# Head norms of a recurrent layer: sums kept in 18 rows, factors spread by a store and repeated-row loads in place of matrix products

## The reference, cut to what matters

```python
kk = (k * k_k).reshape(B, T, H, E)
kk = kk / jnp.maximum(jnp.sqrt(jnp.sum(kk * kk, axis=-1, keepdims=True)), 1e-12)
...
mean = jnp.mean(y, axis=-1, keepdims=True)
var = jnp.mean(jnp.square(y - mean), axis=-1, keepdims=True)
yn = (y - mean) * lax.rsqrt(var + LNX_EPS) * lnx_w.reshape(H, E) + lnx_b.reshape(H, E)
```

## Time and profile before

| | |
|---|---|
| runs | 1655.82, 1649.14, 1655.05 us, median 1655.05 |
| profiled execution | 1649.22 us, its span 1647.4 us |
| TensorE busy | 1530.8 us, 93% of the span |
| VectorE / ScalarE / GpSimd busy | 678.1 / 425.5 / 54.8 us |
| mean granted TensorE clock | 0.979 of full |
| recurrent part | from about 63 to 620 us |

### The profile page before, as it was taken

How to read it: one execution, slowest core, us unless ns; L and a number is a source line. 1 busy time by engine, 2 the same in 40 slices (tenths; PEclk the granted TensorE clock), 3 DMA queues, 4 the chain that set the end, 5 groups by cost and what they waited for, 6 DMA issues and landing times. The chain is left out here.

```text
span 1647.4 us, 32642 instructions
## 1 busy us (share of the span) xinstructions
PE 1530.8 (93%) x13954; PEld 1038.5 (63%) x13954; DVE 678.1 (41%) x1669; ACT 425.5 (26%) x876; POOL 54.8 (3%) x57
## 2 busy tenths in 40 slices
PE   7898999999999998998989989999999999995997
PEld 4565676676776656675766664555786777772442
DVE  5456375466455225325152452324552111113554
ACT  4411414313422212314132240113111111111444
POOL 0000000000000000000000000000110011002110
PEclk9999999999999999999999999999999999997998
DMA  5100000100010107405243284004699999995321
GB/s 197 29 27 2 26 17 16 41 15 16 16 42 10 42 10 304 193 16 208 100 194 128 92 346 167 39 26 179 245 359 351 383 375 372 382 397 189 102 90 45
DMA packets 55606, 238.39 MB, mean 145 GB/s; under 512 B 7584, under 2 KB 18080, under 8 KB 45728
## 3 DMA queue, kind: packets, MB, share of 16 engines
q1 hardware_dynamic: 45776, 201.63, 32.1%
q0 software_dynamic: 6176, 22.02, 4.3%
q10 hardware_dynamic: 3504, 12.58, 1.9%
HBM read 206.53 MB, written 29.69 MB: 143 GB/s over the span
## 5 line engine op out<-in xcount | busy, mean ns | idle before, releaser
L466 PE MATMUL bank<-h,w 128*128 128x352 f32 (+1 forms) x528 | 183.8, 496 | 0.0
L466 PEld LDWEIGHTS bank<-h,w 128*128 128x128 f32 x528 | 100.2, 199 | 55.5 <-issue 7.4
L1942 PEld LDWEIGHTS bank<-cache,we 128*128 128x128 f32 x1088 | 125.0, 194 | 11.8 <-issue 7.2
L1942 PE MATMUL bank<-cache,we 128*128 128x96 f32 (+1 forms) x1088 | 126.3, 277 | 3.4 <-DVE cache L2273 3.4
L2273 DVE COPY cache<-bank 128x512 f32<-128x512 f32 (+1 forms) x54 | 31.6, 626 | 217.4 <-PE bank L1921 217.1
L2551 PE MATMUL bank<-we,unT 128*128 128x512 f32 x256 | 112.9, 599 | 1.4 <-DVE unT L2502 1.4
L1864 PE MATMUL bank<-cache,mixed 128*128 128x512 f32 x256 | 112.7, 599 | 0.0
L1354 PE MATMUL bank<-h,w 128*128 128x352 f32 (+1 forms) x288 | 88.4, 469 | 0.0
L2551 PEld LDWEIGHTS bank<-we,unT 128*128 128x128 f32 x256 | 48.6, 193 | 59.5 <-issue 57.8
L1864 PEld LDWEIGHTS bank<-cache,mixed 128*128 128x128 f32 x256 | 48.7, 193 | 58.7 <-issue 58.7
L1964 PE MATMUL bank<-we,gated 128*96 128x512 f32 (+2 forms) x192 | 79.5, 595 | 0.0
(11 more groups left out here) (427 smaller groups left out, 2561.1 us busy)
## 6 DMA issues: line engine op xcount, KB each, us to landing
we<-in_weg SPq DMA_DIRECT2D x24, 1024.0 KB, 14.8
we<-in_weu SPq DMA_DIRECT2D x24, 1024.0 KB, 17.8
we<-in_wed SPq DMA_DIRECT2D x24, 1024.0 KB, 20.3
cache<-in_kcj SPq DMA_DIRECT2D x4, 5120.0 KB, 16.1
cache<-in_vcj SPq DMA_DIRECT2D x4, 5120.0 KB, 15.7
cache<-in_weg SPq DMA_DIRECT2D x8, 1024.0 KB, 15.6
cache<-in_weu SPq DMA_DIRECT2D x8, 1024.0 KB, 18.9
cache<-in_wed SPq DMA_DIRECT2D x8, 1024.0 KB, 19.9
```

The costliest lines, as they stand in the source:

```text
L466: mm = pe.matmul(out[:, 0:w], w3[:, KIND[q], kd, :], g.uT[:, kd, a:a + w], start=(kd == 0), stop=(kd == KD - 1))
L1942: mm = pe.matmul(bank[6 + u % 2][:, 128 * (2 * a + f):128 * (2 * a + f) + CAPS[e]], weights[load_of[e] % NW][a][:, k, 128 * f:128 * f + 12 ...
```

## The change

In the stages that have an own pair (j = 0 to 3) both norms are made in another form; the first and the last stage keep the old one.

- `sums_in_rows`: the squares stream (128 columns a block) over a strip of zeros with one column of ones per head, shifted by one column from block to block, so all nine blocks accumulate into one bank: row tt holds head 0's sums of block tt, row 9 + tt head 1's. Scaling, root and reciprocal work on [18, 128].
- `spread_rows` on SP: when the reciprocal is made, two stores put the 2 x 9 rows into DRAM; when these have landed, two loads bring each head's 1088 values to its 64 partitions, the same DRAM row read 64 times.
- Norm rows lie in `tmp`, their spread in `bv`; key rows in `bv`, their spread in `tmp`. DVE multiplies once over 1088 columns from there. The reuse brings waits: ACT waits for the norm stores before it squares the keys into `tmp`, and for the norm multiplication and the key stores before it evicts into `bv`.
- On SP the norm's trip stands behind the load of k weights, the key's behind the store of output rows (and a small load), and ahead of the loads of r and v weights.
- On DVE the key reciprocal moves ahead of the `z16` read and the second r shift ahead of the key multiplication. PE loses its waits for `d_rec`, `a_rec` and `d_bcx` in these stages.

```diff
@@ sync
+                def spread_rows(rows, out, made, n, stored, landed):
+                    sp.wait_ge(s[made], n)
+                    sp.dma_start(g.rows[0, :, :], rows[0:TT, :]).then_inc(s[stored], 16)
+                    sp.dma_start(g.rows[1, :, :], rows[TT:2 * TT, :]).then_inc(s[stored], 16)
+                    uses[stored] += 32
+                    sp.wait_ge(s[stored], uses[stored])
+                    for h in range(2):
+                        row = g.rows[h, :, :].rearrange("a t -> (a t)")[0:T].unsqueeze(0)
+                        sp.dma_start(out[hs(h), :], row.broadcast_to([E, T])).then_inc(s[landed], 16)
...
                     if jn is not None:
                         next_w3("k", jn)
+                    if jp is not None and j < J:
+                        spread_rows(norm_rows, norm_spread, "d_rec", jp + 1, "n_stored", "n_landed")
                     if jp is not None:
                         sp.wait_ge(s["g_ev"], 3 * jp + 3)
                         sp.dma_start(g.rw[128 * jp:128 * jp + 128, :], cen).then_inc(g.rw_out, 16)
...
+                    if jn:
+                        sp.wait_ge(s["n_landed"], 32 * j)
+                        spread_rows(key_rows, key_spread, "a_rec", jn + 1, "k_stored", "k_landed")
@@ tensor
+                def sums_in_rows(of, out):
+                    order = (0, TT - 1) + tuple(range(1, TT - 1))
+                    for tt in order:
+                        n = rows_of(tt)
+                        mm = pe.matmul(out[0:2 * TT, 0:n], strip[:, TT - 1 - tt:3 * TT - 1 - tt], of[:, 128 * tt:128 * tt + n],
+                                       start=(tt == order[0]), stop=(tt == order[-1]))
+                    return mm
...
-                            head_sums(squares, bank[3]).then_inc(s["d_var"], 1)
-                    if behind:
+                            (sums_in_rows if own else head_sums)(squares, bank[3]).then_inc(s["d_var"], 1)
+                    if behind and not own:
                         pe.wait_ge(s["d_rec"], jp + 1)
                         for part in range(3):
                             spread(stat, bank[NORM_SPREAD[part]], part).then_inc(s["d_bc"], 1)
...
-                        if ahead and n == 3:
+                        if ahead and not own and n == 3:
                             pe.wait_ge(s["a_rec"], jn + 1)
...
@@ scalar
+                        if behind:
+                            act.wait_ge(s["n_stored"], 32 * (jp + 1))
                         act.activation(tmp[:, :], kk[:, :], ACT.Square).then_inc(s["a_sq"], 1)
...
                     if own:
+                        if behind:
+                            act.wait_ge(s["d_bcx"], jp + 1)
+                        if ahead:
+                            act.wait_ge(s["k_stored"], 32 * jn)
                         side(("bv", 0))
@@ vector
+                    if behind and own:
+                        dve.wait_ge(s["n_landed"], 32 * (jp + 1))
+                        dve.scalar_tensor_tensor(out=cen[:, :], in0=cen[:, :], scalar=param("lnx_w", jp), in1=norm_spread, op0=ALU.mult,
+                                                 op1=ALU.mult).then_inc(s["d_bcx"], 1)
...
+                        if own:
+                            shift_in(jn, "r", 1)
+                            dve.wait_ge(s["k_landed"], 32 * jn)
+                            dve.tensor_tensor(kk[:, :], kk[:, :], key_spread, ALU.mult)
```

More of the change, by code:

```diff
@@ L283, in rwkv @@
         w0s = sb("w0s", [128, 2, NB, NT])
-        stat, kstat = (g.mixed[:, spare + a:spare + a + 2 * TT] for a in (0, 2 * TT))
+        stat = kstat = g.mixed[:, spare:spare + 2 * TT]
+        strip = g.mixed[:, spare + 2 * TT:spare + 2 * TT + 3 * TT - 1]
         rest = sb("rest", [128, 3 * J])
@@ L608, in between @@
                     jn, jp = after(j), before(j)
-                    ahead, behind = jn is not None, jp is not None
+                    ahead, behind, own = jn is not None, jp is not None, 0 <= j < J
                     def group(n):
@@ L655, in between @@
                             pe.wait_ge(s["a_sq"], jn + 1)
-                            if behind:
-                                pe.wait_ge(s["d_bcx"], 3 * jp + 1)
-                            head_sums(tmp, bank[7]).then_inc(s["a_ss"], 1)
-                        if ahead and n == 3:
+                            (sums_in_rows if own else head_sums)(tmp, bank[7]).then_inc(s["a_ss"], 1)
+                        if ahead and not own and n == 3:
                             pe.wait_ge(s["a_rec"], jn + 1)
-                            if behind:
-                                pe.wait_ge(s["d_bcx"], 3 * jp + 3)
                             for part in range(3):
@@ L920, in between @@
                         act.wait_ge(s["d_eps"], jp + 1)
-                        act.activation(stat[:, :], stat[:, :], ACT.Sqrt).then_inc(s["d_root"], 1)
+                        rows = norm_rows if own else stat[:, :]
+                        act.activation(rows, rows, ACT.Sqrt).then_inc(s["d_root"], 1)
                     if own:
@@ L940, in between @@
                         act.wait_ge(s["a_max"], jn + 1)
-                        act.activation(kstat[:, :], kstat[:, :], ACT.Sqrt).then_inc(s["a_root"], 1)
+                        rows = key_rows if own else kstat[:, :]
+                        act.activation(rows, rows, ACT.Sqrt).then_inc(s["a_root"], 1)
                     if own:
@@ L1093, in between @@
                         dve.wait_ge(s["d_root"], jp + 1)
-                        dve.reciprocal(stat[:, :], stat[:, :]).then_inc(s["d_rec"], 1)
+                        rows = norm_rows if own else stat[:, :]
+                        dve.reciprocal(rows, rows).then_inc(s["d_rec"], 1)
                     if own:
@@ L1099, in between @@
                         keys(jn, 2)
+                    if behind and own:
+                        dve.wait_ge(s["n_landed"], 32 * (jp + 1))
+                        dve.scalar_tensor_tensor(out=cen[:, :], in0=cen[:, :], scalar=param("lnx_w", jp), in1=norm_spread, op0=ALU.mult,
+                                                 op1=ALU.mult).then_inc(s["d_bcx"], 1)
+                    elif behind:
+                        for n, (a, w) in enumerate(SPANS):
+                            dve.wait_ge(s["d_bc"], n + 1)
+                            dve.scalar_tensor_tensor(out=cen[:, a:a + w], in0=cen[:, a:a + w], scalar=param("lnx_w", jp),
+                                                     in1=bank[NORM_SPREAD[n]][:, 0:w], op0=ALU.mult, op1=ALU.mult)
                     if behind:
[L1101 to L1104 removed]
                         dve.drain()
@@ L1115, in between @@
                         dve.wait_ge(s["a_ss"], jn + 1)
-                        dve.tensor_scalar(kstat[:, 0:16], bank[7][:, 0:16], 1e-24, None, ALU.max)
-                        dve.tensor_scalar(kstat[0:64, 16:18], bank[7][0:64, 16:18], 1e-24, None, ALU.max).then_inc(s["a_max"], 1)
+                        if own:
+                            dve.tensor_scalar(key_rows, bank[7][0:2 * TT, 0:128], 1e-24, None, ALU.max).then_inc(s["a_max"], 1)
+                        else:
+                            dve.tensor_scalar(kstat[:, 0:16], bank[7][:, 0:16], 1e-24, None, ALU.max)
+                            dve.tensor_scalar(kstat[0:64, 16:18], bank[7][0:64, 16:18], 1e-24, None, ALU.max).then_inc(s["a_max"], 1)
                         shift_in(jn, "r", 0)
+                    if ahead:
+                        dve.wait_ge(s["a_root"], jn + 1)
+                        rows = key_rows if own else kstat[:, :]
+                        dve.reciprocal(rows, rows).then_inc(s["a_rec"], 1)
                     if own:
                         last_chunk("z16", 1)
-                    if ahead:
-                        dve.wait_ge(s["a_root"], jn + 1)
-                        dve.reciprocal(kstat[:, :], kstat[:, :]).then_inc(s["a_rec"], 1)
                     if own:
@@ L1126, in between @@
                     if ahead:
-                        for n, (a, w) in enumerate(SPANS):
-                            dve.wait_ge(s["a_nb"], 3 * jn + n + 1)
-                            dve.tensor_tensor(kk[:, a:a + w], kk[:, a:a + w], bank[KEY_SPREAD[n]][:, 0:w], ALU.mult).then_inc(s["a_nbx"], 1)
+                        if own:
+                            shift_in(jn, "r", 1)
+                            dve.wait_ge(s["k_landed"], 32 * jn)
+                            dve.tensor_tensor(kk[:, :], kk[:, :], key_spread, ALU.mult)
+                        else:
+                            for n, (a, w) in enumerate(SPANS):
+                                dve.wait_ge(s["a_nb"], n + 1)
+                                dve.tensor_tensor(kk[:, a:a + w], kk[:, a:a + w], bank[KEY_SPREAD[n]][:, 0:w], ALU.mult)
                         dve.drain()
                         dve.tensor_tensor(tmp[:, :], kk[:, :], icl[:, :], ALU.mult)
-                        shift_in(jn, "r", 1)
+                        if not own:
```

(6 more changed lines are left out.)

18 lines of the change are left out of this document (10 added, 8 removed).

## The result

The changed kernel takes 1662.4 us (median of 20 executions, 1652.52 to 1667.36); before, measured as often, takes 1652.7 us (1646.99 to 1658.52). The ratio is 1.0054, 95% interval 1.0039 to 1.007: slower by about 9 us, where 1649.4 us was forecast with a range up to 1659. The profiled execution of the changed kernel took 1658.66 us against 1649.22 us of the profiled one before.

The account below looks back on a forecast made before the run. PE's instruction stream was taken as the bound, 93% busy. Keys -6.5, norms +1.1 - 2.2 + 2.5 and sums -0.6 gave -5.7 us, from the median 1655.05 to 1649.4 us, range 1640 to 1659.

Parts of the forecast that it names:

- The sum: Whole kernel: keys -6.5, norms of j = 1, 2, 3 +1.1, -2.2, +2.5, sums -0.6, together -5.7 us.
- the structure: Norm trips: DVE waits at its 1088-column multiplication and PE behind it in j = 1 and 3, not in j = 2.
- the covered stage: Norm of j = 2: the trip is all hidden with 1.5 us to spare, -2.16 us.
- The key half: Keys in j = 0, 1, 2: trips covered by PE's own work, 3 x -2.16 = -6.5 us.
- stalls cost clock: Rival, chance 0.14: PE's stalls in j = 1 and 3 drop its clock, 1.7 us each, 1652.8 us.
- the trip: SP's stores and repeated-row loads after the reciprocal: 5.9 us, between 5.0 and 12 us.
- the repeated-row loads are slow: Rival, chance 0.13: the trip takes 6 us more, giving +10.4 us, 1665.5 us.
- The estimate of 5.7 us beside the sum: The trip's chain by the Trainium skill's DMA figures with second issues; would make the sum 0.4 us lower.
- removed products: Six spreads dropped from PE, keys j = 0 to 2 and norms j = 1 to 3: 6 x 2.16 = 13.0 us gain.
- products kept PE slow: Rival, chance 0.14: after key sums of j = 1 and 2, 128-column sums could keep the clock, -3.4 us, 1646.0 us.

Follow-up runs that it names:

- bare delays: Four kernels: the kernel before with idle VectorE operations ahead of the third gm pair in stage 1, 3 or both, no trip; +5.9, +7.4, +12.9 and +29.5 us.
- best1: The changed kernel with norms new in stages 1 and 2 only, where SP issues the norm trip ahead of the k weights; 1645.58 us, ratio 0.997.
- nospread: The kernel before with only the key half changed and the norm spread products of stages 1 to 3 left out, no trip replacing them; 1642.06 us, ratio 0.995.
- nowait: The changed kernel with all transfers, but VectorE's norm multiplication in stages 1 to 3 reads an old tile instead of awaiting loaded rows; 1642.77 us, ratio 0.9951.
- n3only: The changed kernel with norm factors by the trip in stage 3 alone, by products in stages 1 and 2; 1652.99 us, ratio 1.0007.
- pair_first: The changed kernel with VectorE's third gm pair ahead of the wait for loaded norm rows in stages 1 to 3; 1655.22 us, ratio 1.0023.
- norm_only: The kernel before with only the output norms of stages 1, 2 and 3 in the new form, keys old; 1660.36 us, ratio 1.007.
- layout: The kernel before with the change's DRAM tensor and four semaphores allocated and never used; 1649.93 us, ratio 0.9999.
- keys_only: The kernel before with only the key norms of stages 0, 1 and 2 in the new form, output norms old; 1645.17 us, ratio 0.997.
- best3: The changed kernel with norm trips ahead of weights in stages 1 and 2, third pair before stage 3's norm wait, first pair before decay's subtraction; 1645.62 us, ratio 0.9958.
- stall_3: The kernel before with five idle VectorE operations ahead of the third gm pair in stage 3 alone; +7.4 +- 2.5 us.
- dvestall: The kernel before with five idle VectorE operations ahead of the third gm pair in stages 1 and 3; +12.9 +- 3.4 us.

## Why the prediction was wrong

The sum said -5.7 us and the measured difference is +9.7. (The three runs shown of before have a median of 1655.05, the longer series 1652.7; this base was 2.4 us high, so the forecast time looks nearer than the sum was.) Three terms failed; by size the third is the largest.

**Right: the structure.** DVE waits at its 1088-column multiplication in j = 1 and 3 and not in j = 2, PE stands at the successor of L572 in the same two, the covered stage is covered. The prediction named the stalls as 3.3 and 4.7 us; they are 4.06 and 6.01. The reciprocal takes 0.93 us (0.95 forecast), the sums hold PE for 1.96 us (285.87 to 287.83; 1.87 to 2.04 forecast). In j = 1 DVE had the rows at 303.04 (302.5 forecast), in part by luck: the loads took 1.3 us more than forecast, but the stores had landed 0.6 us earlier. DVE's wait at the key multiplication is 1.1 us in one stage and PE has none behind it. The key half was to bring 6.5 us and brought 5.3 +- 1.9.

**Wrong, first: the stalls' clock was left out of the sum.** I had the mechanism as a rival (*stalls cost clock*, chance 0.14, 1.7 us for each of two) and took for the forecast that a stall costs its length. The bare delays show length and a quarter: 2.5 us for the 10.07 us of standing here. The evidence was in the earlier trace rows, one window of two after a 2.4 us wait, and stalls of 3 to 5 us are longer than those. That rival belonged in the sum. Alone it would not have saved the forecast: its own figure was 1652.8, still 2.3 us under the base.

**Wrong, second: the trip was sized too short.** The loads were put at 3.8 us from their first issue, from single transfers in the earlier trace rows, and took 5.06 in j = 1 and 5.6 in j = 3; the trip of j = 3 took 7.2 us (537.58 to 544.78) after a start at once. This is 0.8 and 1.3 us more standing, 2.1 together. It is the rival *the repeated-row loads are slow* in its size, not in its cause: 64 different rows took 4.8 and 5.1 us as well. What was left out is that a pair of such loads takes longer than one. The estimate of 5.7 us beside the sum has the same gap; its fit (Trainium skill, "DMA: Bandwidth & Descriptors", "Anatomy of one DMA") is given there for transfers issued by GpSimd, and SP issued these. j = 2 had the spare for it.

**Wrong, third: removed products were credited in full to the span.** Each kernel from which norm spreads went came out above its sum. The sum here is -5.3 for the keys as measured, -2.16 for each norm spread gone, and 1.24 us for each us of standing added in its trace:

| kernel | spreads, standing | by the sum | measured | above |
|---|---|---|---|---|
| best1 | 2, none | -9.6 | -4.7 +- 2.4 | 4.9 |
| nospread | 3, none | -11.8 | -8.3 +- 3.6 | 3.5 |
| nowait | 3, none | -11.8 | -7.6 +- 2.5 | 4.2 |
| n3only | 1, 5.1 | -1.2 | +1.1 +- 2.5 | 2.3 |
| pair_first | 3, 6.4 | -3.9 | +3.8 +- 1.8 | 7.7 |
| norm_only (no keys) | 3, 9.0 | +4.7 | +10.6 +- 3.1 | 5.9 |
| the change | 3, 10.1 | +0.7 | +9.7 | 9.0 |

So with my forecast's terms put right (+2.5 clock, +2.1 trip, +1.2 keys) the change would stand near zero, and about 9 us remain. nospread and nowait point to 3.5 to 4.2 of them coming with the removal itself and not with the trips, though with intervals of 3.6 and 2.5 us. The other 5 or so appear only where PE also stands behind the trip: taking the waits away brought 17.3 us, the same standing by bare delays costs 12.9. With the scatter of the three kernels that surplus is 4 us give or take 4, so I can't call it shown. Most of it is lost clock: the rest of the changed kernel is only 1.6 us under before, but its lost clock 11.5 above, though the single traces place the dips in different windows from one kernel to the next. (Bare delays of that length bring 4.8 us of it.)

The traces show where the time goes missing. When PE begins the attention's first product (L1363, at 620.8 us in before), the seven kernels of the table lie 0.4 us under their sums in the mean (best1 -12.2, nospread -10.9, nowait -11.3, the change +1.7, each against before's trace), and at the end of the span 7.0 above. Six kernels with the old norms (before, layout, the four with bare delays) lie 1.7 under and 0.4 above. One trace tells this no better than to some 4 us, as layout shows, 4.6 ahead at that place with nothing changed; but in the mean some 5 of 6.6 us go behind the recurrent part, where the change has no instruction. **What stays open** is why. The lost clock from 960 us on is 23.3 us in the mean of the seven and 20.9 in that of the six. That PE reaches other short waits sooner is not what the traces show: its waits from 60 to 650 us other than the one at L572 sum to 29.6 us in before, 27.9 in keys_only and nospread, 29.1 in nowait.

Two kinds of standing have grown outside the edit. One is PE's wait for expert weights at L1989; the other is gaps of PE in which it waits for nothing that the profile shows, the two longest of them here:

```profile
PE bank L1989 <- DMA we<-in_weu: 4.9, 1, 4.9
...
PE bank L767 <- issue: 1.9, 1, 1.9
...
PE bank L1476 <- issue: 1.3, 1, 1.3
```

For the weights keys_only, best1, nospread, nowait and best3 wait 3.3, 4.0, 4.3, 5.2 and 5.4 us, n3only and norm_only 2.4 and 2.5; before has 1.8, layout and the bare delays 2.1 to 2.4. The gaps without a releaser sum to 5.4 us in the change, 6.5 in nowait, 5.5 in nospread, 4.5 in best1, 2.8 in keys_only, and to 0.7 to 3.0 us in the six kernels with the old norms and keys; none of those six has one above 0.7 us, each of the twelve others has one of 1.1 us or more. Against keys_only, from which the sums of the table start, both kinds together are 5.6 us more in nowait, 3.7 in nospread, 2.4 in best1 and 4.2 in the change: that is as much as is missing in the first two, half of it in the others. In pair_first, n3only and norm_only they explain little. It is not clock, and it comes without a trip (nospread) as with it; what makes the gaps no run here shows.

## What to carry to other kernels

A step taken off a saturated TensorE is worth its row at most, and only if nothing is put where it stands; a round trip through DRAM of store, wait and two loads was 6.4 to 7.2 us here where nothing held SP, and the test is whether the engine that asks for it has that much other work first, stage by stage: it had in j = 2 and for all keys, in j = 1 only with the trip issued ahead of the weight load (best1), and it had not in j = 3. Price a stall of TensorE above its length, here by a quarter, and look for the old ones first: moving one VectorE operation behind a read that TensorE waits for gave 6 to 10 us, no less than the better half of the change (5.3). A wait pushed behind one consumer of a block reappears at the next when TensorE wants the whole block (5.3 us at the attention product for 6.0 at the transposes).

## What the runs showed that I had not expected

- Lost clock and rest are separable from every execution's span and mean clock, and the first carries most of the scatter and here the result: 52.0 against 40.5 us at nearly equal rest.
- The clock stayed at 2.4 GHz through all 4.06 us of the stall in j = 1 and for the first 3.8 us of that in j = 3; it fell 0.6 us behind the end of the first and 2.2 us ahead of the end of the second. The products behind pay (key sums 3.39 us against 2.03).
- One DRAM row of 4.25 KB read 64 times cost nothing that shows: 4.8 to 5.6 us for the pair of loads, 4.8 and 5.1 with 64 different rows.
- All twelve kernels with a part of the change have a gap of PE of 1.1 to 2.1 us that no semaphore explains, none of the six others one above 0.7 us.
- The rival *products kept PE slow* can't be settled by one pair of traces. Behind the key sums of j = 2 the changed kernel has 1.00 from 435 to 440 and before 0.76; but layout, with the sums of before, has 1.00 there too (the line below), and no fall in j = 1 either. Over all traces, the clock fell right behind the key sums of j = 2 in five of seven kernels whose sums stream 2 columns and in none of eleven whose sums stream 128. That speaks for the rival; but the lost clock of keys_only is only 2.1 +- 1.8 us under that of before, and all eleven have falls between 466 and 522 us instead, where before, layout, stall_3 and dvestall have none from 450 to 540. A fall avoided in one place can come back in another.

```profile
435.00:440.00 5.00, 5.00 (x43) 3.00 (x41) 0.40 (x2) 0.49 (x1) 0.00 (x0) 1.00 0.01 3
```
